# One-hot products in fp32r, four tokens to a set, with the high and low side of the gate in 256 columns; x kept in DRAM

## The reference

```python
def block(xb):                                    # 128 tokens at a time, 256 in all
    q = (xb @ w_query).reshape(128, 8, 2, 128)
    s1 = einsum('thd,kd->thk', q[:, :, 0], keys1); s2 = einsum(..., q[:, :, 1], keys2)
    v1, i1 = top_k(s1, 16); v2, i2 = top_k(s2, 16)
    top, ci = top_k(v1[..., :, None] + v2[..., None, :], 16)
    idx  = i1[ci // 16] * 128 + i2[ci % 16]       # 8 heads x 16 = 128 experts per token
    gate = softmax(top)
    act  = gelu(einsum('td,tkd->tk', xb, expert_u[idx]))
    return einsum('tk,tkd->td', gate * act, expert_v[idx])
x = x + peer_ffn(h2, ...)
```

## Time and profile before

| | us |
|---|---|
| median of 3 runs (2125.94 to 2132.56) | 2127.1 |
| profiled execution, whole | 2125.79 |
| its span in the trace | 2124.0 |
| TensorE busy in it | 2081.0 |
| VectorE busy | 1516.3 |
| ScalarE busy | 979.2 |
| GpSimd busy | 778.2 |
| mean granted TensorE clock | 0.995 |

### The profile page before, as it was taken

How to read it: one execution, slowest core, us unless ns; L and a number is a source line. 1 busy time by engine, 2 the same in 40 slices (tenths; PEclk the granted TensorE clock), 3 DMA queues, 4 the chain that set the end, 5 groups by cost and what they waited for, 6 DMA issues and landing times.

```text
span 2124.0 us, 45783 instructions
## 1 busy us (share of the span) xinstructions
PE 2081.0 (98%) x14382; PEld 1939.6 (91%) x14382; DVE 1516.3 (71%) x3212; ACT 979.2 (46%) x1365; POOL 778.2 (37%) x323
## 2 busy tenths in 40 slices
PE   7999999999999999999989999999999999999997
PEld 6999899999998888899889989999999988888996
DVE  3843169789878888777639341897988788887776
ACT  4744444555544343444356444555554433344443
POOL 5798679400000000244368887783000000003442
PEclk9999999999999999999999999999999999999999
DMA  6455457655568878755444554576445677776553
GB/s 237 139 185 189 149 174 227 211 166 164 161 196 241 242 240 241 217 190 182 167 170 147 186 187 149 183 230 201 162 162 161 214 242 239 242 240 208 187 186 121
DMA packets 154706, 410.71 MB, mean 193 GB/s; under 512 B 16987, under 2 KB 67340, under 8 KB 154588
## 3 DMA queue, kind: packets, MB, share of 16 engines
q1 hardware_dynamic: 154220, 407.75, 60.0%
q0 software_dynamic: 368, 1.57, 0.2%
HBM read 382.00 MB, written 27.26 MB: 193 GB/s over the span
## 4 chain that ended last, share of the span: by engine, by line
PE 96%; ACT 1%; issue 1%; DVE 1%; DMA 0%; DVEq 0%; ACTq 0%
PE bank L1049 55%; PE bank L1250 33%; PE bank L1302 5%; PE bank L1228 1%; PE bank L1071 1%; PE bank L1104 0%; PE bank L1212 0%; PE bank L1151 0%; DVE area L749 0%; DVE hT L756 0%; DMA x<-in_x 0%; ACT area L486 0%; ACT area L541 0%; PE bank L1161 0%; PE bank L1149 0%
## 5 line engine op out<-in xcount | busy, mean ns | idle before, releaser
L444 POOL TENSOR_TENSOR halves<-ring,halves 128x1024 fp32r<-128x1024 f32 x308 | 772.0, 2518 | 1309.6 <-DVE coef L983 943.4
L1049 PE MATMUL bank<-hT,halves 128*128 128x256 f32 x8688 | 1122.0, 286 | 9.9 <-DVE hT L756 8.1
L510 ACT ACTIVATE halves<-ring 128x1024 fp32r<-128x1024 f32 x668 | 707.3, 1060 | 873.9 <-PE bank L1049 470.1
L1049 PEld LDWEIGHTS bank<-hT,halves 128*128 128x128 f32 x8688 | 1068.9, 191 | 18.4 <-issue 9.1
L1250 PE MATMUL bank<-halves,coef 128*128 128x512 f32 x3072 | 709.2, 390 | 0.0
L1250 PEld LDWEIGHTS bank<-halves,coef 128*128 128x128 f32 x3072 | 572.3, 188 | 117.3 <-DVE coef L983 0.9
L944 DVE TENSOR_TENSOR halves<-ring,halves 128x1024 fp32r<-128x1024 f32 x360 | 443.0, 1231 | 67.3 <-ACT x L650 25.8
L977 DVE TENSOR_TENSOR act<-act,area 128x256 f32<-128x256 f32 x256 | 219.6, 858 | 88.9 <-ACT act L620 85.5
L957 DVE TENSOR_SCALAR onehot<-ids,x 128x128 f32<-128x128 f32 x512 | 177.2, 346 | 1.9 <-issue 1.9
L956 DVE TENSOR_SCALAR x<-ids,x 128x128 f32<-128x128 f32 x512 | 146.4, 286 | 16.5 <-PE bank L1302 15.6
L1302 PE MATMUL bank<-onehot,x 128*128 128x128 f32 x1024 | 156.1, 274 | 0.0
(11 more groups left out here) (138 smaller groups left out, 946.8 us busy)
## 6 DMA issues: line engine op xcount, KB each, us to landing
ring<-in_stream SPq DMA_DIRECT2D x672, 512.0 KB, 3.4
held_blocks<-act SPq DMA_DIRECT2D x188, 128.0 KB, 1.9
act<-held_blocks SPq DMA_DIRECT2D x188, 128.0 KB, 3.1
area<-rel_scratch SPq DMA_DIRECT2D x2, 1024.0 KB, 6.4
rel_scratch<-act POOLq DMA_DIRECT2D x1, 1532.0 KB, 14.5
area<-in_consts SPq DMA_DIRECT2D x2, 576.0 KB, 3.8
x<-in_x SPq DMA_DIRECT2D x1, 1024.0 KB, 4.9
out_y<-x SPq DMA_DIRECT2D x2, 512.0 KB, 2.7
```

Of the source, the lines that this page charges most:

```text
L444: pool.tensor_tensor(halves[:, s, 1, :], ring[:, s, :], halves[:, s, 0, :].bitcast(F32), ALU.subtract)\
L510: a.activation(halves[:, s, 0, :], ring[:, s, :], ACT.Copy).then_inc(hi_done, 1)
L1049: i = pe.matmul(o, stationary[a], moving[b], start=begin and n == 0, stop=end and n == len(TERMS) - 1)
```

## The change

- One-hots are built for a *set* of 4 tokens; there are 64 sets per layer and two slots. All one-hots are fp32r. The weight is split in a high and a low side, so `onehot2` has 256 columns a token: mask x high weight, and mask x low weight. One matmul per token gives both sides of its slice, in one half of a bank; four banks (2 to 5) take turns.
- VectorE makes a set with whole-set operations: `hi` = (key 2 == column number) for 4 tokens (512 columns), `onehot1` for 2 tokens and then 2 more (256 each), `lo` = mask x low weight (512), and `hi` x high weight for the first 2 tokens (256). ScalarE multiplies the other 2 tokens (`weighted`). Keys and weights are read from PSUM (banks 0 and 1), where TensorE's transposes left them; `weight_low` and a rounded weight are written there once per layer.
- ScalarE copies the high side of a finished pair of tokens to the table (`side`); VectorE adds the low side from PSUM (`add_side`), after it has built the next set.
- One `u` block goes with each set: 64 in the one-hot stage (`HELD`), so `EARLY` is 112 and `MAIN` is 16. GpSimd now makes all low halves up to the V stage.
- x is stored to DRAM (`x_home`, 1 MB, issued by ScalarE behind `roots`) and loaded back in the main stage by the SP queue. The accumulators are no longer opened with x: the first `v` product opens them, and the end of the layer adds (`tensor_tensor`) instead of copying.
- The loop over layers and the one-hot stage are written out (Python loops) on all engines.

```diff
-STEPS = 4
-BODY = 32
+FOUR = 4
+SETS = S // FOUR
-HELD = 48
+HELD = 64
...
+        onehot1 = coef[:, :, :, :].rearrange("p k a t -> p (k a t)").rearrange("p (b u k) -> p b u k", b=2, u=FOUR)
+        onehot2 = nc.alloc_sbuf_tensor_at("onehot2", [P, 2, FOUR, 2, NK], F32R, offset=x_base)
-        bank_g = bank[4:6]
+        bank_g = bank[2:6]
+        key1T, key2T = (bank[0][:, c * S:(c + 1) * S] for c in range(2))
+        weightT, weight_low = (bank[1][:, c * S:(c + 1) * S] for c in range(2))
...
 (SP)
-            with sp.Fori(0, DEPTH) as l:
+            for l in range(DEPTH):
-                        sp.wait_ge(lo_vector, l * LOV + r * RING + (s + 2))
+                        sp.wait_ge(lo_pool, l * LOP + r * RING + (T_HU + s + 2))
                         load(r * RING + (T_HU + RING + s), s, l)
+                sp.wait_ge(outer_done, (l + 1) * NQ)
+                sp.dma_start(x[:, :, :], x_home).then_inc(x_loaded, 16)
...
 (ScalarE)
                 roots(l * NSCAL + 9, ...)
+                a.dma_start(x_home, x[:, :, :]).then_inc(x_saved, 16)
                 high_rows("h2T")
...
+                def weighted(n):
+                    a.wait_ge(low_placed, l * SETS + n + 1)
+                    for u in range(2, FOUR):
+                        rows = onehot2[:, n % 2, u, 0, :]
+                        i = a.activation(rows, rows.bitcast(F32), ACT.Copy, scale=weight[:, n, u - 2:u - 1])
+                    i.then_inc(onehots_ready, 1)
+                def side(q):
+                    a.wait_ge(outer_done, l * NQ + q + 1)
+                    a.activation(gates_t[:, :, 2 * q:2 * q + 2],
+                                 bank_g[q % 4][:, :].rearrange("p (t h e) -> p h e t", t=2, h=2)[:, 0], ACT.Copy)
+                for n in range(SETS):
+                    if n >= 1:
+                        side(2 * n - 2)
+                        side(2 * n - 1)
+                    if n + 1 < SETS:
+                        weighted(n + 1)
+                    hold(n)
...
 (VectorE)
+                def add_side(q):
+                    v.wait_ge(side_copied, l * NQ + q + 1)
+                    g2 = gates_t[:, :, 2 * q:2 * q + 2]
+                    v.tensor_tensor(g2, g2, bank_g[q % 4][:, :].rearrange("p (t h e) -> p h e t", t=2, h=2)[:, 1], ALU.add)
+                def onehots(n):
+                    if n >= 2:
+                        v.wait_ge(outer_done, l * NQ + 2 * (n - 1))
+                    v.tensor_tensor(hi, keys2, numbers, ALU.is_equal).then_inc(mask_ready, 1)
+                    v.tensor_tensor(onehot1[:, n % 2, 0:2], keys1[:, 0:2], numbers[:, 0:2], ALU.is_equal)
+                    v.wait_ge(mask_ready, l * SETS + n + 1)
+                    v.tensor_tensor(lo, hi.bitcast(F32), low_weights, ALU.mult).then_inc(low_ready, 1)
+                    v.tensor_tensor(onehot1[:, n % 2, 2:4], keys1[:, 2:4], numbers[:, 2:4], ALU.is_equal)
+                    v.wait_ge(low_ready, l * SETS + n + 1)
+                    v.tensor_tensor(hi[:, 0:2], hi[:, 0:2].bitcast(F32), weightT..., ALU.mult).then_inc(low_placed, 1)
+                onehots(0)
+                onehots(1)
+                for n in range(1, SETS):
+                    if n + 1 < SETS:
+                        onehots(n + 1)
+                    add_side(2 * n - 2)
+                    add_side(2 * n - 1)
-                            v.tensor_scalar(onehot1[:, s, u, :], iota, key1, None, ALU.is_equal)
-                            i = v.tensor_scalar(onehot2[:, s, u, :], iota, key2, weight, ALU.is_equal, ALU.mult)
...
-                        v.tensor_copy(x[:, t, hf * HALF_N:(hf + 1) * HALF_N], acc[2 * t + hf][:, :])
+                        v.tensor_tensor(xs, xs, acc[2 * t + hf][:, :], ALU.add)
...
 (TensorE)
-                for t in range(TT):
-                    for hf in range(2):
-                        pe.matmul(acc[2 * t + hf][:, :], ident, x[:, t, hf * HALF_N:(hf + 1) * HALF_N], start=True, stop=True)
+                for n in range(SETS):
+                    held(n)
+                    pe.wait_ge(onehots_ready, l * SETS + n + 1)
+                    for q in (2 * n, 2 * n + 1):
+                        if q >= 4:
+                            pe.wait_ge(table_ready, l * NQ + q - 3)
+                        for u in range(2):
+                            pe.matmul(bank_g[q % 4][:, u * S:(u + 1) * S], onehot1[:, n % 2, row, :], onehot2[:, n % 2, row]...)
```

More of the change, by code:

```diff
@@ L78 @@
 MAIN = NK - EARLY
-CHUNKS = 3
 EXP_AT = 8
 SEL_AT = 2
-PER = BODY * CHUNKS // KD
-assert PER * (S // 2 // BODY) == HELD and PER % RING == 0
+assert SETS == HELD
 HIS = NT - 2
-LOP = T_HU + MAIN
-LOV = BESIDE + NK
+LOP = T_PV + MAIN
+LOV = NK
 TERMS = ((0, 0), (0, 1), (1, 0))
@@ L173, in program @@
         stat = sb("stat", [P, 16])
+        weight = sb("weight", [P, SETS, 2])
         used = [0]
@@ L450, in low @@
                 subtract(s)
-            with pool.Fori(0, DEPTH) as l:
+            for l in range(DEPTH):
                 pool.wait_ge(params_ready, l + 1)
@@ L462, in _ @@
                 i.then_inc(wsp_ready, 1)
-                with pool.Fori(1, T_HU // RING) as r:
+                with pool.Fori(1, T_PV // RING) as r:
                     for s in range(RING):
@@ L499, in roots @@
                 i.then_inc(root_ready, 1)
-            a.sem_inc(table_ready, 2)
             a.wait_ge(chain, 1)
-            with a.Fori(0, DEPTH) as l:
+            for l in range(DEPTH):
                 g = [0]
@@ L659, in hold @@
                     gelu(i % 2)
-                with a.Fori(0, NQ // BODY) as j:
-                    def table(g4):
-                        a.wait_ge(outer_done, l * NQ + j * BODY + (STEPS + 2 * (g4 + 1)))
-                        a.activation(gates_t[:, :, bass.ds(j * (2 * BODY) + 4 * g4, 4)],
-                                     bank_g[g4 % 2][:, :].rearrange("p (t e) -> p e t", t=4), ACT.Copy)\
-                            .then_inc(table_ready, 1)
-                    for q in range(BODY):
-                        if q % 2:
-                            table(q // 2)
-                        for c in range(CHUNKS * q, CHUNKS * (q + 1)):
-                            if c % KD == KD - 1:
-                                hold(j * PER, c // KD)
+                def weighted(n):
[4 more added lines that the diff above has]
+                    i.then_inc(onehots_ready, 1)
@@ L675, in _ @@
+                side(NQ - 2)
+                side(NQ - 1)
                 for i in range(TAIL):
-                    hold(HELD, i)
+                    hold(HELD + i)
                 with a.Fori(0, EARLY // RING) as r:
@@ L717, in _ @@
             v.tensor_copy(relv, bank[0][:, 0:NDIST]).then_inc(rel_vector, 1)
-            with v.Fori(0, DEPTH) as l:
+            for l in range(DEPTH):
                 links = [1]
@@ L941, in low @@
+                onehots(0)
[5 more added lines that the diff above has]
+                    add_side(2 * n - 1)
+                add_side(NQ - 2)
+                add_side(NQ - 1)
                 def low(n, s):
@@ L1016, in _ @@
         def _(pe):
-            pe.sem_inc(outer_done, STEPS)
             pe.wait_ge(consts_loaded, 16)
@@ L1023, in _ @@
             pe.wait_ge(rel_vector, 1)
-            with pe.Fori(0, DEPTH) as l:
+            for l in range(DEPTH):
                 g = [0]
@@ L1209, in _ @@
                 pe.wait_ge(taken_v, l * NGV + taken_before(first("h2T"))[0])
-                for t in range(TT):
-                    for hf in range(2):
-                        pe.matmul(acc[2 * t + hf][:, :], ident, x[:, t, hf * HALF_N:(hf + 1) * HALF_N], start=True,
-                                  stop=True)
                 pe.wait_ge(diag_ready, l * 2 + 2)
@@ L1275, in _ @@
                         for t in range(TT):
-                            b = group("sel")
-                            for c in range(3):
-                                i = pe.transpose(b[:, c * P:(c + 1) * P], sel[:, c, t, :], ident)
-                            i.then_inc(groups_done, 1)
+                            for c, o in enumerate((key1T, key2T, weightT)):
+                                i = pe.transpose(o[:, t * P:(t + 1) * P], sel[:, c, t, :], ident)
+                        i.then_inc(sel_turned, 1)
@@ L1300, in _ @@
+                for n in range(SETS):
[4 more added lines that the diff above has]
+                            pe.wait_ge(table_ready, l * NQ + q - 3)
                         for u in range(2):
-                            o = (2 * q + u) % 4 * NK
-                            i = pe.matmul(bank_g[g4 % 2][:, o:o + NK], onehot1[:, s, u, :], onehot2[:, s, u, :],
-                                          start=True, stop=True)
+                            row = 2 * (q % 2) + u
+                            i = pe.matmul(bank_g[q % 4][:, u * S:(u + 1) * S], onehot1[:, n % 2, row, :],
+                                          onehot2[:, n % 2, row].rearrange("p h k -> p (h k)"), start=True, stop=True)
@@ L1304, in _ @@
```

(8 more changed lines are left out.)

120 lines of the change are left out of this document (66 added, 54 removed).

## The result

| | before | after |
|---|---|---|
| median | 2126.52 us (4 runs) | 2077.4 us (4 runs: 2073.36, 2073.94, 2080.87, 2082.28) |
| profiled execution | 2125.79 us | 2073.36 us, span 2071.4 |
| ratio of the times | | 0.9764, 95% interval 0.9732 to 0.9797 |

The change takes 49 us off, 2.4%.

A forecast was written before the change was run, and what follows sets the result against it. TensorE was taken as the only bound, VectorE next. From the profiled 2125.8 us, 2125.8 - 50.0 - 0.6 - 0.8 + 4.6 = 2079.0; with the median 1.3 above the profiled run, 2080 us, range 2073 to 2104.

The forecast's parts named there:

- TensorE's part: One-hot stage: 256 products a layer go from 0.2175 to 0.1199 us each, 50.0 us gained in all.
- Moved blocks: 16 `u` and `v` blocks a layer leave the main stage for the one-hot and V stages: 0.6 us gained.
- VectorE in a set: One-hot stage: VectorE's seven operations a set take 2.83 to 3.46 us, 2.83 taken, against TensorE's 3.36.
- Written-out loops: Layer boundary: without the jump ScalarE loads its table while TensorE finishes, 0.8 us gained, once.
- The clock behind the openings: Behind the wo products: TensorE idles 4.2 us without the openings, the clock falls, 4.6 us lost in two layers.
- x in DRAM: Store of x behind `roots` and reload in the main stage: costed at 0, at 4 x 3.1 us if in the way.
- the VectorE case: Rival: VectorE becomes the bound of the one-hot stage, 13 to 26 us more, 2093 to 2106 us; chance 0.15.
- The slower one: Rival: GpSimd holds VectorE's new set operations, 1.93 us a hold, one a set, 179 us, about 2255; chance 0.05.

The follow-up runs named there:

- after_again: The changed kernel run once more, with nothing changed, against the kernel before: 2075.94 us, ratio 0.9749.
- extra1: The changed kernel with one more VectorE operation (a sum over 256 columns of the keys in PSUM) in every set: 2076.0 us.
- extra3: The changed kernel with three more VectorE operations (sums over 256 columns of the keys in PSUM) in every set: 2137.42 us, ratio 1.0045.
- before_layers_out: The kernel before with only the loop over the two layers written out on all five engines: 2122.18 us, ratio 0.997.
- cover: The changed kernel with the four ident x x products back behind the wo products, their result not used: 2071.01 us.
- lo_sbuf: The changed kernel with one set operation (`lo`) reading its second operand from SBUF instead of PSUM: 2078.13 and 2084.63 us.
- warm: The changed kernel with 9 products of constants behind the wo products and 12 at the layer boundary: 2071.82 us.

## Why the prediction was right

The forecast was 2080 us, 2073 to 2104, and the median is 2077.4. The mechanism held: TensorE was the bound and stayed it, and its products became cheaper by what the `u` row said. That the median is as near as 2.6 us is in part luck. It lies between the two pairs of runs, where no run is; the changed kernel's other job, after_again, has a median of 2075.9, and for the profiled execution the sum said 2079.0 where 2073.4 was measured. Step by step:

- *TensorE's part*, 50.0 us: right in mechanism, the size is 512 x (0.221 - 0.1205) = 51.5. The new product costs 0.1205 us (3.36 - 2.88 = 0.48 for four), as the `u` row said. The Trainium skill, FP8 and Floating Point Precision, section TensorE Precision Notes, gives four passes for true fp32; the estimate worked out from that was 0.109 for one pass of 256 columns, and this trace is a tenth above it. The old one cost 0.221, not 0.2175: the window that I took for the stage ends nine `u` matmuls before its last block does, so 1.1 us of one-hot products went to the blocks. The period of 1.52 us gives 0.220 and would have been the better row.
- *Moved blocks*, 0.6: 1.1 us (V and main stage with 16 blocks' `u` products added, 441.50 to 440.96 a layer).
- *VectorE in a set*, 2.83 us: 2.99 us, without a stall of TensorE. Overlap is as taken; the rest is `add_side` at 0.444 instead of 0.418 and the hand-overs. extra1 and extra3 show that this is the second bound, 0.37 us away.
- *Written-out loops*, 0.8: the boundary gave 0.9. The sum has nothing for the front, 1.8 us here, and before_layers_out gained 3.6 us in all; how much of either is the loops' is open, since the front differs by as much between executions of kernels that all have them written out.
- *The clock behind the openings*, 4.6 lost: 2.7 in the profiled execution (1.0 and 1.7), 3.8 behind the openings of after_again, and 4.9 by the medians of cover and after_again. The place is as charged; the size was too high for the profiled execution. The Trainium skill, TensorE: Matmul & The Clock Gate, section Why this matters for your kernels, warns against idle gaps between bursts of matmuls. This trace agrees: an idle gap of 4.27 us in the middle of busy matmuls was followed by the low level, and without the gap, in cover, it was not.
- *x in DRAM*, 0: the reload is issued at 946.6 us, lands 8.1 us later, and TensorE has no wait in the main stage; cover, which has the store, takes 10.25 us from the opening to the second half of the `q` products, before_layers_out, which has none, 10.26. So nothing, as charged.
- *The rivals*: the VectorE case was ruled out by extra1. The slower one (GpSimd holds VectorE) took 1.93 us a hold, and lo_sbuf shows 2.1, but its one hold in each set was one in five, and VectorE's slack took in most of them: one operation that can be held costs 1.0 to 1.4 us a layer, not 90. The reason to give it only 0.05 was right, the 179 us were not. (Added to 2080 they make 2259, not 2255, and the rivals' own chances leave 0.91 for faster, not 0.92; neither bears on the forecast.)

For the profiled execution the sum was 5.6 us high: 1.5 from the products, 0.5 from the blocks, 0.1 from the boundary, 1.8 from the front that it did not have, and 1.9 from the clock that it charged too dear. The step from there to the median was put at 1.3 us and is 4.0, because two of the four runs are dear; that took half of the error back.

## What to carry to other kernels

Where TensorE is the bound, price a product by a row of the same type and column count, and take the old price from a period of the timeline, not from a window whose edges cut a block. When an edit removes work of the bounding engine in front of a wait, look at what the wait becomes: here products whose result nobody needs are worth 1.9 to 2.5 us a layer, because they keep the clock up, and as many more of them as run past the end of the wait cost their own time (0.45 us a layer in warm). Count the next engine's slack a period (0.37 us here) before adding to it. Before giving a gain to the change, look whether that stretch is as long in a second trace of the same kernel: 1.8 us of the difference here is not.

## What the runs showed of the hardware that I had not expected

- The low clock level can outlast the idle time by far. In lo_sbuf's profiled run TensorE was busy without a gap and the clock stayed at 0.50 for 17 us (7.4 us lost); in the profiled run of before it was back within 4 us of the same place. The traces do not show what decides.
- A VectorE operation with two SBUF inputs and a GpSimd subtraction hold each other both ways: 2.82 us for 0.68 of VectorE in one set, 2.75 us for 2.41 of GpSimd in the next. In a loop where both recur every 3.36 us they met in nearly every set, but VectorE was the one held in 25 of 128 only, and GpSimd in 99 of 126.
- The same two subtractions of VectorE at the start of the program took 3.62 us in one execution and 4.98 in another (4.70 in extra1), and the next products started 1 us apart. A difference of 1 to 2 us there says nothing of two kernels until more traces show it.
- An fp32r product takes 0.110 us with 128 columns and 0.1205 with 256; an fp32 one 0.221 and 0.430.
